# Order of the products in the first branch unit, and place of the last sliding-window head's values, in a hybrid attention layer

## The reference

```
o_s = swa_sink_attention(q_s, k_s, v_s, swa_sinks)      # 8 heads of 64, window of 128
o_f = forgetting_attention(q_f, k_f, v_f, f_l + b_forget)  # 8 heads of 64, causal
gates = sigmoid(g + b_gate)                              # (512, 2, 1024)
merged = gates[:, 0] * (o_s @ w_branch_swa) + gates[:, 1] * (o_f @ w_branch_fox)
return merged @ w_out
```

## Time and profile before

| | |
|---|---|
| time, median of 3 runs | 1243.81 us (1243.01 to 1245.15) |
| profiled execution, its own time | 1243.32 us |
| span of its trace | 1241.6 us |
| PE busy | 1220.1 us, 98% of the span |
| DVE busy | 803.2 us, 65% |
| ACT busy | 501.8 us, 40% |
| mean granted clock of PE | 0.997 of full speed |

### The profile page before, as it was taken

One profiled execution on the slowest core, in us unless ns is written; L12 is line 12 of the kernel. 1 busy time (PEld: TensorE's weight loads), 2 busy tenths in 40 slices (PEclk: granted clock), 3 DMA queues, 4 the chain that ended last, 5 costly groups with the idle time before them and its releaser, 6 DMA issues.

```text
span 1241.6 us, 16266 instructions
## 1 busy us (share of the span) xinstructions
PE 1220.1 (98%) x6003; PEld 1026.0 (83%) x6003; DVE 803.2 (65%) x1128; ACT 501.8 (40%) x789; POOL 134.5 (11%) x148
## 2 busy tenths in 40 slices
PE   8999999999999999999999999999999999999996
PEld 7888888888888888888878888888988888888885
DVE  5374747474977776677754477555747474747497
ACT  5242424242435666566643315442324242424241
POOL 1201010101223100011010020001310101010112
PEclk9999999999999999999999999999999999999998
DMA  9938383838477322222263515213573838383741
GB/s 291 302 86 220 84 220 84 220 82 222 79 214 234 92 79 59 78 56 64 57 216 100 187 34 177 78 52 119 171 185 87 219 84 220 84 220 84 220 85 68
DMA packets 180550, 171.19 MB, mean 138 GB/s; under 512 B 6016, under 2 KB 151440, under 8 KB 179472
## 3 DMA queue, kind: packets, MB, share of 16 engines
q1 hardware_dynamic: 165136, 126.92, 33.6%
q0 software_dynamic: 15152, 43.52, 16.4%
q10 hardware_dynamic: 208, 0.01, 0.0%
HBM read 137.93 MB, written 7.34 MB: 117 GB/s over the span
## 4 chain that ended last, share of the span: by engine, by line
PE 89%; DVE 4%; DMA 2%; ACT 2%; issue 1%; POOL 1%; SPq 0%; DVEq 0%; POOLq 0%; ACTq 0%
PE bank L884 19%; PE bank L885 19%; PE bank L886 19%; PE banks_scores L885 9%; PE banks_scores L884 9%; PE banks_scores L886 9%; DMA wd<-in_mem_w_k 1%; PE bank L1232 1%; DVE ring_lo L1878 1%; PE bank L904 1%; DMA raw<-in_ffn_w_gate 1%; PE bank L1252 1%; ACT prob L1709 1%; PE bank L1251 0%; PE banks_scores L1202 0%
## 5 line engine op out<-in xcount | busy, mean ns | idle before, releaser
L884 PE MATMUL bank<-xT_hi,ring_hi 128*128 128x512 f32 (+1 forms) x728 | 279.1, 383 | 1.8 <-DVE ring_lo L1878 1.8
L886 PE MATMUL bank<-xT_hi,ring_lo 128*128 128x512 f32 (+1 forms) x728 | 276.8, 380 | 0.0
L885 PE MATMUL bank<-xT_lo,ring_hi 128*128 128x512 f32 (+1 forms) x728 | 276.7, 380 | 0.0
L1878 DVE TENSOR_TENSOR ring_lo<-raw,ring_hi 128x1024 fp32r<-128x1024 f32 x171 | 207.6, 1220 | 50.1 <-ACT ring_hi L1466 49.4
L1466 ACT ACTIVATE ring_hi<-raw 128x1024 fp32r<-128x1024 f32 x171 | 179.6, 1057 | 145.5 <-PE bank L886 113.4
L884 PEld LDWEIGHTS bank<-xT_hi,ring_hi 128*128 128x128 f32 x728 | 137.0, 188 | 26.7 <-issue 2.0
L886 PEld LDWEIGHTS bank<-xT_hi,ring_lo 128*128 128x128 f32 x728 | 136.9, 188 | 26.4
L885 PEld LDWEIGHTS bank<-xT_lo,ring_hi 128*128 128x128 f32 x728 | 137.1, 188 | 24.5
L884 PE MATMUL banks_scores<-xT_hi,ring_hi 128*128 128x512 f32 (+1 forms) x384 | 142.8, 372 | 0.0
L886 PE MATMUL banks_scores<-xT_hi,ring_lo 128*128 128x512 f32 (+1 forms) x384 | 142.6, 371 | 0.0
L885 PE MATMUL banks_scores<-xT_lo,ring_hi 128*128 128x512 f32 (+1 forms) x384 | 142.6, 371 | 0.0
(11 more groups left out here) (357 smaller groups left out, 2088.0 us busy)
## 6 DMA issues: line engine op xcount, KB each, us to landing
raw<-in_ffn_w_gate SPq DMA_DIRECT2D x44, 512.0 KB, 6.7
raw<-in_ffn_w_up SPq DMA_DIRECT2D x44, 512.0 KB, 5.9
wd<-in_ffn_w_down SPq DMA_DIRECT2D x20, 1024.0 KB, 5.2
raw<-in_mix_w_in SPq DMA_DIRECT2D x34, 512.0 KB, 3.8
t<-in_ffn_w_down SPq DMA_DIRECT2D x20, 512.0 KB, 6.7
t<-wd POOLq DMA_DIRECT2D x11, 512.0 KB, 5.2
wd<-wd POOLq DMA_DIRECT2D x10, 512.0 KB, 8.1
t<-t POOLq DMA_DIRECT2D x10, 512.0 KB, 9.6
```

The costliest lines, as they stand in the source:

```text
L884: pe.matmul(dst, hi, mhi, start=start, stop=False)
L885: pe.matmul(dst, hi, mlo, start=False, stop=False)
L886: return pe.matmul(dst, lo, mhi, start=False, stop=stop)
L1878: nc.vector.tensor_tensor(dst, src, hi.bitcast(F32), ALU.subtract).then_inc(done, 1)
```

## The change

Three things change. The first branch unit of each gate (u == 2) takes k = 0, 1, 2 of both column blocks first and k = 3 of both last, and waits for three pairs at its start and for the fourth ahead of its last six matmuls. Head 7's values move from behind `scores(8)` into the middle of the project unit U_G0 + 1, as those of other heads stand. And its chain moves with it: on ACT `output_other(7)` and `pair_high(3)` go between the weight split of that unit and its `gate_tanh`; on DVE `output_sum(7)` and `pair_low(3)` go to the start of step 9, behind the normalization of head 8, `stack_low(9)` and a weight split.

```diff
-            def branch(n, o, b_hi, b_lo):
+            def branch(n, o, b_hi, b_lo, pairs_done, first=False):
                 ready(n)
                 hi, lo = (r.rearrange("p (k c) -> p k c", k=4) for r in parts(n))
-                for e in range(2):
-                    proj_is_out(pe, o + e - 2)
+                if first:
+                    order = [(e, k) for e in range(2) for k in range(3)] + [(0, 3), (1, 3)]
+                    pe.wait_ge(o_lo, pairs_done - 1)
+                else:
+                    order = [(e, k) for e in range(2) for k in range(4)]
+                for e, k in order:
+                    if k == 0:
+                        proj_is_out(pe, o + e - 2)
+                    if first and (e, k) == (0, 3):
+                        pe.wait_ge(o_lo, pairs_done)
                     cols = slice(e * P, (e + 1) * P)
-                    for k in range(4):
-                        mm = split_product(bank((o + e) % 2), ...)
-                    mm.then_inc(*((branch_full, 1) if e == 0 else (unit_used, 1)))
+                    mm = split_product(bank((o + e) % 2), ...)
+                    if k == 3:
+                        mm.then_inc(*((branch_full, 1) if e == 0 else (unit_used, 1)))
...
  PE, heads:
-                    if H >= 2 and H != SWA_HEADS + 1:
+                    if H >= 2:
                         values(H - 2)
...
-                        pe.wait_ge(o_lo, SWA_HEADS // 2)
-                        branch(U_G0 + u, O_G0 + 4 * (u // 3) + 2, os_hi, os_lo)
+                        branch(U_G0 + u, O_G0 + 4 * (u // 3) + 2, os_hi, os_lo, SWA_HEADS // 2, u == 2)
...
                 scores(H)
-                if H == SWA_HEADS:
-                    values(H - 1)
...
  PE, second gate:
-                    pe.wait_ge(o_lo, HEADS // 2)
-                    branch(U_G1 + u, o, of_hi, of_lo)
+                    branch(U_G1 + u, o, of_hi, of_lo, HEADS // 2, u == 2)
...
  ACT:
-                    if H >= 2 and H != SWA_HEADS + 1:
+                    if H >= 2:
                         output_other(H - 2)
...
+                            if u == 1:
+                                pair_high((H - 3) // 2)
                             gate_tanh(n, o, 0, m)
                 if H >= 1:
                     copied_probs(H - 1)
-                if H == SWA_HEADS:
-                    output_other(H - 1)
-                    pair_high((H - 1) // 2)
                 exponentials(H, at_swa if H < SWA_HEADS else FOX_AT, H if H < SWA_HEADS else None)
...
  DVE:
-                        if H >= 2 and H != SWA_HEADS + 1:
+                        if H >= 2:
                             output_sum(H - 2)
+                        if H == SWA_HEADS + 1:
+                            pair_low((H - 3) // 2)
...
-                elif H == SWA_HEADS:
-                    output_sum(H - 1)
-                    pair_low((H - 1) // 2)
                 normalize_probs(H, at, sink)
```

More of the change, by code:

```diff
@@ L1174, in project_out @@
                 project(n, bank(o % 2), between=between)
-            def branch(n, o, b_hi, b_lo):
+            def branch(n, o, b_hi, b_lo, pairs_done, first=False):
                 ready(n)
                 hi, lo = (r.rearrange("p (k c) -> p k c", k=4) for r in parts(n))
-                for e in range(2):
-                    proj_is_out(pe, o + e - 2)
+                if first:
[8 more added lines that the diff above has]
+                        pe.wait_ge(o_lo, pairs_done)
                     cols = slice(e * P, (e + 1) * P)
-                    for k in range(4):
-                        mm = split_product(bank((o + e) % 2), hi[:, k, cols], lo[:, k, cols], b_hi[:, k, :], b_lo[:, k, :],
-                                           k == 0, k == 3)
-                    mm.then_inc(*((branch_full, 1) if e == 0 else (unit_used, 1)))
+                    mm = split_product(bank((o + e) % 2), hi[:, k, cols], lo[:, k, cols], b_hi[:, k, :], b_lo[:, k, :],
+                                       k == 0, k == 3)
+                    if k == 3:
+                        mm.then_inc(*((branch_full, 1) if e == 0 else (unit_used, 1)))
             def t_bank(n):
```

## The result

The changed kernel takes 1246.47 us in the median of 22 executions (1244.65 to 1249.32), the kernel before 1243.55 us in 22 beside it. The ratio is 1.0022, 95% interval [1.0016, 1.0027]: some 2.7 us slower by the ratio (the two medians lie 2.9 us apart), just beyond the 0.2% that the prediction called indistinguishable. The prediction had the sign and a cost of 1.1 us; its range ended at 1246.4 us, within 0.1 us of the median and of the profiled execution of the changed kernel (1246.40 us).

The account below looks back on a forecast made before the run. The prediction took PE, busy 98% of the span, as the bound. A first-gate cost of 1.8 us less a second-gate gain of 0.74 gave +1.1 us, from 1243.81 to 1244.9 us, range 1243.3 to 1246.4.

Parts of the forecast that it names:

- The removed waits: First gate: the 1.0 us wait before head 7's values vanishes; the branch unit begins at 538.68, a gain of 1.13 us.
- The moved chain: First gate's branch unit: the tanh behind `pair_high(3)` delays block 1; PE stands 2.6 to 3.0 us, net cost 1.64 to 2.02.
- One aside: First gate's branch unit: with its order left alone, block 1 would be wanted only 0.7 us later.
- The second gate: Second gate's first branch unit: the wait for the eighth pair's low half goes; gain 0.74 us, bounded by 1.68 and 0.
- both small waits of the forecast: Second gate: new waits for block 1's tanh and block 0's eviction, near ties of 0.28 and 0.34 us.
- The sum: Whole kernel: +1.8 us in the first gate less 0.74 in the second gives +1.1 us, 1244.9 us; chance 0.69.
- The clock: Rival: the first gate's stall drops PE's clock to 1.2 GHz, losing 1.4 to 2.8 us; 1247.0 us, chance 0.07.
- the prediction's own list of signs: Profile signs of being wrong: `gate_tanh` ahead of the sum, PE not standing there, or the granted clock dropping after 543.
- half a microsecond of spread: Allowance for the spread of the runs, a half microsecond at each end of the range.
- Block 1 not waiting: Rival, first gate: the chain is quicker and PE does not wait; 1241.9 us, chance 0.09.
- the second gate giving nothing: Rival: the second gate's two small waits grow and its 0.74 us gain becomes 0; 1245.6 us, chance 0.13.
- the side to which 0.09 was given: Whole kernel: the outcome of being slower by over 0.2% (2.49 us), chance 0.09.

Follow-up runs that it names:

- second profile of the changed kernel: The changed kernel, unaltered, profiled again when re-timed beside the filled one on one chip: 1247.01 us, ratio 1.0023; profiled execution 1246.68 us.
- experiment 1: The changed kernel with the tanh put ahead of `pair_high` on ACT: ratio 0.9991, 1243.14 us against 1243.86.
- experiment 3: The kernel before with the new order of products in the first gate alone, head 7's values and chain left in place: ratio 1.0003.
- experiment 7: The changed kernel with the old order and full wait in the first gate's first branch unit, values still moved: ratio 1.0044, 1249.09 us.
- the filled kernels: The changed kernel with 12 or 6 unused matmuls added ahead of block 1's wait: 12 took 1245.03 us and, repeated, 1245.20; 6 took 1245.07.
- experiment 5: The changed kernel with 6 unused matmuls added ahead of block 1's wait: ratio 1.0011, 1245.07 us.
- experiment 8: The changed kernel with head 7's chain pulled ahead on ACT and DVE and the tanh first in step 9: ratio 0.9981, 1241.77 us.
- experiment 6: The changed kernel and its version with 12 unused matmuls, re-timed on one chip: 1247.01 us (ratio 1.0023) and 1245.20 us (1.0008).
- experiment 10: The changed kernel with head 7's chain pulled ahead, and old order with later fourth-pair wait in the second gate: ratio 0.9978, 1241.03 us.

## Why the prediction was right in the mechanism and small in the size

*The removed waits.* Right. The branch unit of the first gate begins at 538.90, forecast 538.68 and 0.21 for the later start of this execution. That the two agree to 0.01 us is in part luck: the project unit began 0.1 us earlier than forecast (532.36 against 532.25 + 0.21) and took 0.1 us longer (6.54 against 6.43).

*The moved chain.* Right, at the upper end. From `ntop` to the sum it took 541.93 - 535.05 = 6.88 us, one of the two values of the earlier trace rows. Block 1 began at 543.98; the forecast's upper end with the offset was 543.92. At full clock, as in the second profile of the changed kernel, the whole unit takes 8.60 us; from a start at 538.90 it would end at 547.50, 2.03 us later than before, where 1.64 to 2.02 was forecast. Experiments 1 and 3 put the cause where the prediction had it: on the tanh queued behind `pair_high`, once the chain is late. One aside was wrong: that with the order within the unit left alone PE would stand only 0.7 us less. In experiment 7 it stands for 5.07 us instead of 2.88, because the old order waits for all four pairs at its start.

*The second gate.* Right: 0.75 us against 0.74, with both small waits of the forecast there.

*The sum.* +1.1 is what the filled kernels measured (ratios 1.0010, 1.0011, 1.0008), whose clock did not fall at the stall in the profiled executions: about 1.2 us. The forecast of 1244.9 us is also where the seven executions of the changed kernel at a mean clock of 0.997 lie (1244.65 to 1245.28).

*The clock.* This is the step that failed. The prediction had the fall as its slow rival, with 1.4 to 2.8 us, and gave it a chance of 0.07. It cost 1.61 us where it came, and the mean clocks and the medians say that it came often. By the prediction's own list of signs, a drop of the clock after 543 meant that it was wrong, and the clock dropped at 544.3. The prediction read two rows, 1.75 us of idle without a fall and a fall 2.8 us after the last matmul, put the new stall of 2.5 to 2.8 us between them, and then took "at the edge" for "unlikely". A stall that ends at the very length at which the only fall shown had come deserved, in our judgement, a chance near one half. The stall came out at 2.88 us by the trace, with the fall right behind it. The total of +1.1 and 1.6 is the 2.7 us of the ratio. The range left this case out, and that its upper end still comes within 0.1 us of the median is luck: that end (1246.3 by its own terms, given as 1246.4) was built from a second gate that gains nothing and half a microsecond of spread, and neither is what happened.

By the Trainium skill, page "TensorE: Matmul & The Clock Gate", Part 1, an idle spell brings the half rate back and sustained work lifts it. The trace of the changed kernel agrees on both: 0.50 behind the stall, and back at 1.00 after 3.4 us of matmuls.

*The chances.* Block 1 not waiting (0.09) and the second gate giving nothing (0.13) are both excluded by the trace. The measured 0.22% is on the side to which 0.09 was given.

## What to carry to other kernels

A wait is paid by whatever stands behind it in the same queue. When a step is moved to a later place on an in-order engine, look for the first instruction behind it that frees a buffer, and put that one first if its input is ready. Spreading an operand's use over both output blocks makes one block's bank wanted earlier and the other's end later; when the missing operand comes soon, a later wait in the old order gives more. A stall of the matmul engine can have two prices, itself and a lower clock behind it. Here idle stretches from 2.6 us on mostly had both, and the second (1.6 us) was over half of the first (2.9 us).

## What the runs showed of the hardware

In the same kernel the clock falls in one execution and not in another. Around the stall of the first branch unit, idle of 1.5 us (experiment 5) was followed by full clock; one stretch of 2.88 us ended with a fall, one of 2.87 us did not. The idle time until the fall is not fixed either. In experiment 7 PE stood for 5.07 us and the windows show 1.00 until 544, 5 us after the idle began, so the fall came only when the work did.

The start of the program, ahead of the first product with weights, shows the same in all 13 profiled executions. In nine of them PE's idle stretch there was 1.46 to 2.33 us, and the clock stayed at 1.00. In four it was 2.58, 2.60, 2.71 and 2.80 us (experiments 8, 6, 10 and 5), and the clock fell each time. These are the timeline and the windows of experiment 10:

```profile
6.94 1.69 PE L969 MATMUL bank<-ident_b 128*128 128x256 bf16 x14
11.34 0.35 PE L884 MATMUL bank<-xT_hi,ring_hi 128*128 128x256 f32 x1 [2.71 <-DVE ring_lo L1887]
```

```profile
13.00:14.00 1.00, 1.00 (x6) 1.00 (x6) 0.00 (x0) 0.00 (x0) 0.00 (x0) 0.50 1.02 371
...
15.00:16.00 1.00, 1.00 (x8) 1.00 (x7) 0.69 (x1) 0.72 (x2) 0.32 (x1) 0.75 1.20 291
```

and this is the end of the same opening work in the kernel before:

```profile
8.09 1.69 PE L969 MATMUL bank<-ident_b 128*128 128x256 bf16 x14
```

The idle stretch is longer because PE was done with the transposition of x and the identity matmuls behind it 1.15 us earlier (8.63 against 9.78), while the product with the first weights began at nearly the same time (11.34 against 11.54). PE being early in one place thus cost it its clock. The scatter of the kernel before (1242.36 to 1245.71 us) goes with the mean clock of each execution, as the figures under experiment 6 show. That the fall at the start makes this scatter is likely, but only profiled executions show where a fall lies. How often it comes for a stall of a given length stays open for the same reason: there are two profiled executions of the changed kernel.
